# Expert rows added straight into the outputs, bias rows made in the projection, meta products in strips, attention's third gate behind the first scores

## What is computed

```python
p = rms_norm(h) @ w_in            # q,f,v,g of HGRN2; q,k,v of attention; two merge gates
o_rec = hgrn2_scan(...)           # recurrence in chunks, state 4 x 128 x 128 per stream
o_att = attend(q, banded(k), banded(v), bias, valid, sinks)  # 8 heads, window 128 + 16 meta keys
h = h + (sig(g_a)*(rec @ Wb_a) + sig(g_b)*(att @ Wb_b)) @ w_out
# MoE: 4 groups of 8 experts, top-2 of the chosen group, d_ff 512
y = expert_dispatch(rms_norm(h), expert, weight, wg, wu, wd)
y_prompt, y_sample = h + y        # plus new key, value and state caches
```

## Time and profile before

| | us |
|---|---|
| median of 3 runs | 1893.47 |
| the profiled execution, its time | 1892.08 |
| its span, first to last instruction | 1890.2 |
| PE busy | 1690.5 (89%) |
| DVE, ACT, POOL busy | 521.0, 471.1, 164.5 |
| mean granted TensorE clock | 0.95 of full speed |
| DMA moved | 321.98 MB, mean 170 GB/s |

### The profile page before, as it was taken

One profiled execution on the slowest core, in us unless ns is written; L12 is line 12 of the kernel. 1 busy time (PEld: TensorE's weight loads), 2 busy tenths in 40 slices (PEclk: granted clock), 3 DMA queues, 4 the chain that ended last, 5 costly groups with the idle time before them and its releaser, 6 DMA issues. The chain is left out here.

```text
span 1890.2 us, 23561 instructions
## 1 busy us (share of the span) xinstructions
PE 1690.5 (89%) x9059; PEld 811.5 (43%) x9059; DVE 521.0 (28%) x1164; ACT 471.1 (25%) x1095; POOL 164.5 (9%) x164
## 2 busy tenths in 40 slices
PE   7999998999994889999669999964999998999993
PEld 3445654666563345555434554531333332332331
DVE  2111301776764123333212333331211111111110
ACT  2254201445442244545200101010111111111110
POOL 0000000222231000000000000010111111111100
PEclk9999998999997889999779999986999999999997
DMA  4511102010025511100083222146899999999984
GB/s 135 168 45 67 45 1 81 33 34 33 23 66 172 193 57 39 44 35 38 17 312 128 78 90 78 45 177 247 331 390 403 401 400 390 399 400 390 399 306 123
DMA packets 80189, 321.98 MB, mean 170 GB/s; under 512 B 16185, under 2 KB 39905, under 8 KB 66417
## 3 DMA queue, kind: packets, MB, share of 16 engines
q1 hardware_dynamic: 63792, 274.44, 37.5%
q0 software_dynamic: 9792, 31.25, 6.1%
q10 hardware_dynamic: 6512, 15.00, 2.1%
HBM read 284.30 MB, written 46.86 MB: 175 GB/s over the span
## 5 line engine op out<-in xcount | busy, mean ns | idle before, releaser
L1506 PE MATMUL ps<-wg,xt 128*128 128x512 f32 x432 | 201.0, 615 | 4.8 <-DMA wg<-w_in 4.8
L2174 PE MATMUL ps<-eu,xsT 128*32 128x512 f32 x1152 | 173.5, 605 | 10.2 <-DMA fu<-w_expert_up 10.2
L2174 PE MATMUL ps<-eg,xsT 128*32 128x512 f32 x1152 | 173.1, 604 | 4.6 <-DVE hid L2126 3.2
L2174 PE MATMUL ps<-fu,xsT 128*32 128x512 f32 x384 | 173.2, 605 | 0.0
L2174 PE MATMUL ps<-fg,xsT 128*32 128x512 f32 x384 | 172.7, 604 | 0.0
L2174 PE MATMUL ps<-ed,hT 128*32 128x512 f32 x1152 | 169.6, 594 | 1.7 <-ACT hT L2104 1.5
L2174 PE MATMUL ps<-fd,hT 128*32 128x512 f32 x384 | 169.3, 594 | 0.0
L2114 DVE TENSOR_TENSOR xsT<-ps,wnT 128x512 f32<-128x512 f32 x48 | 30.9, 686 | 463.6 <-PE ps L2182 463.6
L261 PE MATMUL ps<-wbuf,wide 128*128 128x512 f32 (+3 forms) x384 | 151.7, 549 | 0.0
L1907 PE MATMUL ps<-wb,wide 128*128 128x512 f32 x288 | 132.4, 614 | 14.0 <-DVE mg L1810 6.2
L1919 PE MATMUL ps<-wo,mgT 128*128 128x512 f32 x288 | 127.2, 595 | 2.8 <-DVE o_lg L1831 2.8
(11 more groups left out here) (320 smaller groups left out, 2172.6 us busy)
## 6 DMA issues: line engine op xcount, KB each, us to landing
eg<-w_expert_gate SPq DMA_DIRECT2D x23, 2048.0 KB, 18.6
eu<-w_expert_up SPq DMA_DIRECT2D x23, 2048.0 KB, 18.3
ed<-w_expert_down SPq DMA_DIRECT2D x23, 2048.0 KB, 18.7
fg<-w_expert_gate SPq DMA_DIRECT2D x8, 2048.0 KB, 21.8
fu<-w_expert_up SPq DMA_DIRECT2D x8, 2048.0 KB, 14.8
fd<-w_expert_down SPq DMA_DIRECT2D x8, 2048.0 KB, 13.8
gt<-g_dram SPq DMA_DIRECT2D x9, 1024.0 KB, 5.7
g_dram<-gb SPq DMA_DIRECT2D x9, 768.0 KB, 3.3
```

Of the source, the lines that this page charges most:

```text
L1506: mm = pe.matmul(ps[2 + (n + j) % 2][:, :], xt[:, n, k * P:(k + 1) * P], wg[:, j, k, :], start=(k == 0), stop=(k == KC - 1))
L2174: last = pe.matmul(bank[c, :], rows[:, c], mine if q < 3 else other, start=start, stop=stop)
```

## The change

Numbers in code are from the kernel before where they stand in both. `...` marks what is left out.

1. **project** also makes the bias rows: it loads the two tables, does the product after the last `hf` job, copies it and writes it to DRAM. The meta tile's `hv` and `akv` products are done in four strips: strip `q` holds the same 16 stationary columns and streams a quarter of the weight columns.

```diff
+                if b == 2:
+                    sp.wait_ge(s_rv, 2)
+                    sp.dma_start(T.relv_dram.rearrange(...), relv[:, :]).then_inc(s_vd, 16)
+                    sp.wait_ge(s_vd, 16)
+                    sp.dma_start(T.V, T.relv_dram.to_broadcast([P, AH * RELS])).then_inc(s_vd, 16)
...
+                elif a == MT:
+                    w4 = n // 4
+                    for k in range(KC):
+                        for q in range(4):
+                            last = pe.matmul(bank[32 * q:32 * q + META, 0:w4], T.xnT[:, k, c0:c1], w(k)[:, q * w4:(q + 1) * w4], ...)
...
+                if j == ends[1] - 1:
+                    pe.matmul(ps[0][0:AH, 0:RELS], table[:, :], onehot[:, :], ...).then_inc(s_rv, 1)
```

```diff
+            sp.dma_start(T.wg0[:, :, :], w_in[:, :, C_GA:C_GA + 512]).then_inc(T.s_wg0, 16)
...
             for h in range(H):
+                if h == H - 1:
+                    store(ST)
                 sp.wait_ge(s_sn, h + 1)
                 sp.dma_start(A.s_sample[0, :, h]..., sst[:, h, :, :]).then_inc(s_sw, 16)
-            store(ST)
             sp.wait_ge(s_gw, 16 * NT)
             sp.wait_ge(s_out, 16)
-            sp.wait_ge(s_sw, 16 * H)
```

```diff
         @block.sync
         def _(sp):
-            sp.dma_start(xt[:, 0, :], T.xn_dram[ST]).then_inc(s_xt[0], 16)
+            sp.wait_ge(T.s_states, 16 * H)
             with nc.allow_non_contiguous_dma(reason="small tables"):
-                sp.dma_start(table[:, :], A.rel_bias_table).then_inc(s_c, 16)
-                sp.dma_start(onehot[:, :], A.c_bucket).then_inc(s_c, 16)
...
-                sp.wait_ge(s_v, 2)
-                sp.dma_start(relv_dram.rearrange("o (h n) -> (o h) n", h=AH), relv[:, :]).then_inc(s_vd, 16)
-                sp.wait_ge(s_vd, 16)
-                sp.dma_start(V, relv_dram.to_broadcast([P, AH * RELS])).then_inc(s_vd, 16)
-                sp.wait_ge(s_vd, 32)
...
+                sp.dma_start(xt[:, 1, :], T.xn_dram[0]).then_inc(s_xt[1], 16)
+                sp.dma_start(cv[:, :, :], A.cache_swa_v[0].rearrange("j w k d -> w j (k d)")).then_inc(s_sv, 16)
...
-            for j, (sem, value) in enumerate(((s_c, 112), (s_vd, 16), (s_vd, 32))):
-                pool.wait_ge(sem, value)
+            for j in range(1, GJ):
+                if j == 2:
+                    pool.wait_ge(s_wg[0], 16)
                 c0 = (C_GA, C_GB)[j % 2] + j // 2 * 512
-                pool.dma_start(wg[:, j, :, :], w_in[:, :, c0:c0 + 512]).then_inc(s_wg if j else s_wg0, 16)
+                pool.dma_start(wg[j][:, :, :], w_in[:, :, c0:c0 + 512]).then_inc(s_wg[j - 1], 16)
...
-            queries(0, reused=False)
-            for j in range(GJ):
-                if j < 2:
-                    pe.wait_ge(s_wg if j else s_wg0, 32 if j else 16)
+            def first_gate(j):
+                pe.wait_ge(s_wg[j - 1] if j else T.s_wg0, 16)
                 for k in range(KC):
                     gate(0, 0, j, k)
+
+            first_gate(0)
+            pe.wait_ge(s_k, 4)
...
+            first_gate(1)
+            pe.wait_ge(s_sc, 16)
...
+            queries(0, reused=False)
+            pe.wait_ge(s_kte, 3)
+            pe.wait_ge(s_sk, 3)
             scores(0, 0, 0)
+            first_gate(2)
             tile(0, 0, first=True)
```

```diff
+                if s == NT - 1:
+                    sp.wait_ge(s_mg, 2 * NT)
+                    e = unit_experts(1)[0]
+                    sp.dma_start(T.eg[1][:, :, :], A.w_expert_gate[0, e].rearrange("(p k) f -> p k f", k=KC)).then_inc(T.s_eg[1], 16)
...
+                    sp.dma_start(T.fu[:, :, :], A.w_expert_up[0, unit_experts(0)[1]].rearrange("(p k) f -> p k f", k=KC)).then_inc(T.s_fu, 16)
...
+                own_slots(sp, 0, NG - 1)
+                shared_slots(sp, 0)
...
+            act.wait_ge(s_sc, 32 * NT)
+                shared_slots(act, 1)
+                shared_slots(act, 2)
+                own_slots(act, NG - 1, NG)
...
+            pool.wait_ge(s_ix, 1)
+            pool.wait_ge(s_ox, 16 * NT)
+            for u in range(2):
+                pool.indirect_dma_start(out=T.xs[:, u, :], ...).then_inc(T.s_xs[u], 16)
```

```diff
                 if u >= 1:
-                    pool.wait_ge(s_add, 16 * u)
-                pool.indirect_dma_start(out=T.acc_dram, ..., compute_op=ALU.add).then_inc(s_add, 16)
+                    pool.wait_ge(s_add, 32 * u)
+                pool.indirect_dma_start(out=A.y_prompt[0], ..., bounds_check=SEQ - 1, oob_is_err=False, compute_op=ALU.add).then_inc(s_add, 16)
+                pool.indirect_dma_start(out=A.y_sample..., ..., bounds_check=P - 1, oob_is_err=False, compute_op=ALU.add).then_inc(s_add, 16)
...
-            sp.wait_ge(s_add, 16 * UNITS)
-            sp.dma_start(A.y_prompt[0], T.acc_dram[0:SEQ]).then_inc(s_out, 16)
-            sp.dma_start(A.y_sample..., T.acc_dram[SEQ:PADS]).then_inc(s_out, 16)
-            sp.wait_ge(s_out, 32)
```

More of the change, by code:

```diff
@@ L265, in _ @@
                     turn(a + 2)
+                if j == ends[1] - 1:
+                    pe.wait_ge(s_tb, 32)
+                    pe.wait_ge(s_xn, MT + 1)
+                    pe.matmul(ps[0][0:AH, 0:RELS], table[:, :], onehot[:, :], start=True, stop=True).then_inc(s_rv, 1)
         @block.scalar
@@ L307, in _ @@
                 r = rows(a) if kind not in ("hf", "hq") else P
-                if kind == "hv":
+                if kind in ("hv", "akv") and a == MT:
+                    dst = T.v if kind == "hv" else T.akv
+                    for q in range(4):
+                        last = act.copy(dst[0:META, MT, q * (n // 4):(q + 1) * (n // 4)], bank[32 * q:32 * q + META, 0:n // 4])
+                    last.then_inc(s_free[j % 4], 1)
+                elif kind == "hv":
                     act.copy(T.v[0:r, a, :], bank[0:r, :]).then_inc(s_free[j % 4], 1)
@@ L477, in recur @@
         s_sw = m.sem("r_sw")
+        T.s_states = s_sw
         whg = T.whg
@@ L1069, in attend @@
         GJ = 3
-        wg = m.sb("wg", [P, GJ, KC, 512])
+        wg12 = m.sb("wg", [P, GJ - 1, KC, 512])
+        wg = [T.wg0] + [wg12[:, j, :, :] for j in range(GJ - 1)]
         xt = m.sb("xt", [P, 2, D])
+        xst = T.mixT[:, 0:2, HW:]
         gb = m.sb("gb", [P, GJ, 512])
         qsq = big[:, 0:AH * HD]
-        s_wg0 = m.sem("a_wg0")
-        s_wg = m.sem("a_wg")
+        s_wg = [m.sem(f"a_wg{j}") for j in range(1, GJ)]
         s_xt = [m.sem(f"a_xt{n}") for n in range(2)]
@@ L1275, in tile @@
                         square(i + 1)
-                        if not first:
-                            gate(i, 2, n)
+                        gate(i, 2, n)
                     elif g == 1:
@@ L1464, in _ @@
         def _(pe):
-            pe.wait_ge(s_c, 112)
-            pe.matmul(ps[3][0:AH, 0:RELS], table[:, :], onehot[:, :], start=True, stop=True).then_inc(s_v, 1)
-            pe.wait_ge(s_k, 4)
-            for t in range(MT + 1):
-                n = META if t == MT else P
-                last = pe.transpose(ps[t // 4][:, (t % 4) * P:(t % 4) * P + n], T.akv[0:n, t, 0:RW], T.eye[0:n, 0:n])
-                if t % 4 == 3 or t == MT:
-                    last.then_inc(s_ktp, 1)
-            pe.wait_ge(s_sc, 32)
-            for j in range(STREAMS):
-                last = pe.transpose(ps[4 + j // 4][:, (j % 4) * P:(j % 4 + 1) * P], ck[:, j, :], T.eye[:, :])
-                if j % 4 == 3:
-                    last.then_inc(s_sk, 1)
-            pe.wait_ge(s_kte, 3)
-            pe.wait_ge(s_sk, 3)
             def queries(i, reused=True):
@@ L1501, in gate @@
                 if k == 0:
-                    if j == 0:
-                        pe.wait_ge(s_xt[n], 8 * (number - n) + 16)
+                    if j == 0 and (not isinstance(number, int) or number):
+                        pe.wait_ge(s_xt[n], 8 * (number - n) + 16 * n)
                     if j >= 2 or not isinstance(number, int) or number:
                         pe.wait_ge(s_ge, GJ * number + j - 1)
-                mm = pe.matmul(ps[2 + (n + j) % 2][:, :], xt[:, n, k * P:(k + 1) * P], wg[:, j, k, :],
+                own = isinstance(number, int) and number == 0
+                x = xst[:, k // 4, k % 4 * P:(k % 4 + 1) * P] if own else xt[:, n, k * P:(k + 1) * P]
+                mm = pe.matmul(ps[2 + (n + j) % 2][:, :], x, wg[j][:, k, :],
                                start=(k == 0), stop=(k == KC - 1))
@@ L1786, in _ @@
                     act.drain().then_inc(s_ex, 1)
+            act.wait_ge(s_sc, 32 * NT)
+            with nc.allow_non_contiguous_dma(reason="slot tables"):
+                shared_slots(act, 1)
+                shared_slots(act, 2)
+                own_slots(act, NG - 1, NG)
         @block.vector
@@ L1990, in experts @@
         s_ix = m.sem("e_ix")
-        s_xz = m.sem("e_xz")
-        s_xs = [m.sem(f"e_xs{n}") for n in range(2)]
+        s_xs = T.s_xs
         s_xp = m.sem("e_xp")
@@ L2022, in _ @@
             sp.dma_start(ids[:, :], A.c_rows).then_inc(s_ids, 16)
-            gate(T.eg[1], own(1), T.s_eg[1])
```

(9 more changed lines are left out.)

244 lines of the change are left out of this document (149 added, 95 removed).

## The result

The changed kernel takes 1847.94 us, the median of four runs (1843.82 to 1849.89), against 1894.26 us before: ratio 0.9747, 95% interval 0.9726 to 0.9767. In five later runs it took 1843.15 us (1841.97 to 1845.23), ratio 0.9728 (0.9710 to 0.9746). So it is 46 to 51 us faster; the forecast was 1828 us with a range up to 1845.

The account below looks back on a forecast made before the run. PE was taken to be busy 1690.5 of 1890.2 us, the rest being waits. Savings of 4.5 + 20.5 + 13.8 + 9 + 18 = 65.8 us gave a span of 1824.4, 1828 us for the median; 8-in-10 range 1814 to 1845.

Parts of the forecast that it names:

- Project: Meta tile's products in strips, 2.6 and 1.8 us for two jobs, and the bias product moved in: 4.5 us saved (3 to 7).
- Attend: Start of attend: SP's list sets the start of the steady tiles and gets shorter; 20.5 us saved (14 to 29).
- rival A: Attend: SP's list doesn't shrink as its waits did, 10 us saved instead of 20.5, 1839 us; A or B in full 20%.
- the reordering: Attend: the new order of the gates is itself hidden behind SP's list.
- Merge to experts: PE's pause between merge and experts: earlier scatter, shorter way to the gather, faster gather; 13.8 us saved (7 to 16).
- The end: After the last add: no copy of the result, last block starts at 1868.3; 18 us saved (16 to 19).
- Inside experts: Experts: 32 unfilled rows less per unit relieve the DMA engines and PE's weight waits; 9 us saved (0 to 14.9).
- the price of the waits: Experts: PE's four waits for shared up weights, 10.2 us, cost 14.9 us together with the slow records after them.
- The reserve for the second add: Experts: the second add's fixed part, two more packets per engine and unit, up to 0.33 us a unit.
- Rival B: Experts limited otherwise: second add eats the saving, or loads come late whatever the bytes; 9 becomes 0, 1837; A or B 20%.
- Merge: Merge: PE's work is the same and five weight loads go out near its end; cost 0, up to +2 us.
- D: Experts: a row left out is moved all the same in an add, 1933 us; with other ways to be slow 4%.

Follow-up runs that it names:

- e15: The changed kernel with the third gate of number 0 ahead of the first scores again, as in the kernel before: 1844.7 us.
- e7: The changed kernel with number 2's input load and number 0's gate store moved ahead of the small value loads and output stores in attend: 1831.3 us.
- e11: The changed kernel with the gathers of units 0 and 1 issued at the start of experts instead of the end of merge: 1840.9 us.
- e12: The changed kernel with rows spread by the vector engine, the early store in attend, and the last unit's adds issued in the last block: 1815.6 us.
- e3: The kernel before with a bound on its one add, so the 32 unfilled rows of each unit are left out: 1894.2 us.
- e10: The kernel before with unfilled rows left out of its one add and an expert's rows spread over the groups of four partitions: 1878.4 us.
- e1: The changed kernel with the second add, to y_sample, left out in every unit: 1843.4 us.
- e2: The changed kernel with a third add in each unit whose 128 rows are all left out: 1844.1 us.
- e5: The changed kernel with both adds of every unit and the waits on them removed: 1818.95 us.
- e9: The changed kernel with an expert's consecutive ranks spread by the vector engine over different groups of four partitions: 1834.7 us.
- e4: The changed kernel with the shared up weights issued ahead of the own gate weights in every third unit of experts: 1846.7 us.

## Why the prediction was wrong

The direction and most steps held; the time was 15 to 20 us too short, and the forecast's range ended between the two medians that were measured (1843.15 and 1847.94).

- **Project**: 5.9 in the first profile, 7.4 in the second (a transpose near recur's end starts at 584.33 before, at 578.46 and 576.91 after). The strips stand at the lower bound: 1.9 and 1.1 us for 2.6 and 1.8, since no round waited for its own weights. The Trainium skill, "TensorEngine Tiling (Array Packing)", section Instruction Overhead, puts some 60 cycles on each matmul whatever its length; the trace does not agree. Halving the columns halved a round (0.109 to 0.055 us), and four products in 0.055 us are 14 ns each, 33 cycles at 2.4 GHz.
- **Attend**: right in size, 19.7 for 20.5, and in mechanism. SP's list set the start: from its first issue to the store it took 54.1 us for 72.1, so 18.0 went for the 20.1 worked out. `far` gave 6.7 us back and `bias`, `sink` and `xt` took 10.1 more, so rival A came true for some 2 of its 10 us. PE stood 11.1 us for "12 to 15". e15 shows that the reordering is hidden, e7 that the store was not.
- **Merge to experts**: 12.3 for 13.8. The terms up to the gather were right. The step said that the two gathers and the blocks' meeting "end at about 1281.5, ahead of that": the meeting does not lie beside the gathers, it waits for them (e11).
- **The end**: 12.9 for 18, by the same omission. That "the last block starts at 1868.3", 3.8 us after the first add's issue, took the meeting for free of the adds; it was 10.0 us (e12 shows it at 0.9 us once no add is out).
- **Inside experts**: the step that failed, 15 us by itself in the first profile and 11 in the second. It read: "32 rows less in each unit save 32 x 0.34/16 = 0.68 us of DMA time". Bytes and price per row were right (in e3, with all 24 adds in the window, q0's share fell by 2.8%; a row takes 0.328 us). So was the price of the waits: 14.9 us worked out, 15.5 gone in e10. The division by 16 was wrong. By e3 against e10, the busiest engine sets the pace of the loads; the engine is set by the partition of the row, and the unfilled rows lay mostly on the other eight. What the pads save there is 30 rows of 1536 on the first eight engines. The reserve for the second add was wrong too: an indirect DMA has 16 small packets and not 32, the others in q0 were one of 4 bytes for each row that a gather leaves out, and at 9 ns each they cost nothing that could be seen (e1, e2). Rival B gave the size (9 becomes 0), for two reasons of which neither was this one; e1 and e2 take away the first, e5, e9 and e10 the second.
- **Merge**: 0 with bounds to +2 was 2.7 in the first profile, with a slow clock in that execution, and 0.7 in the second.

D never happened: a left-out row is a packet of 8 bytes. That the 1848 given for A and B together is the first median is luck: A had a small part and B's reasons none, while the blocks' meetings, merge and the growth of experts, which no rival had, made up the rest.

## What to carry to other kernels

Before pricing bytes taken from a full DMA system, ask which engines they come off: for rows addressed one by one, list the rows per engine over the partitions and look at the largest sum, not at the mean. When a block ends while indirect transfers are out, price their landing as part of every engine's way to the next block, or issue them behind the meeting. And when the list of one issuing engine ends last, look for what in it nobody waits for; moving 34 issues behind one store brought 13.5 us here.

## What was not expected of the hardware

- With adds out, the blocks meet 3 us after the last has landed (landing 5.0 us, meeting 8.2 us after the issue); with gathers out, 5.5 us after the issue of the last, and a gather's landing took 4.2 to 4.4. With none out they meet in 0.3 to 0.9 us (e5, e11, e12).
- A wait for weights kept its total when two loads changed places (e4): 12.1 us for one tensor in four waits, 12.3 us for another in six.
- 16 slot loads of 32 rows of 8 bytes each took ACT's queue 12.25 us, 0.77 us each, where a plain load's issue takes 0.33 to 0.45.
- In an unhindered stretch the weights' queue moved 426 to 437 GB/s (merge from 1203.5 to 1212.5), nearly all of it loads of 16 KB a partition; the slices of experts in which the engines never stood (11 us each, share 1.01 and up) moved 391 to 418.
